# Sample queries stored one block earlier, and 44 ticks of fetched rows in memory attention instead of 35

## The chip, the core and the metric

The kernel runs on one core of one Trainium2 chip. The metric is the device time of one execution in microseconds (us), the median of several runs. One further execution was taken by the hardware profiler; it gives the rows below.

## The reference, cut to what matters

One layer of a decoder works on 1024 prompt positions and on 8 samples of 8 positions each (64 sample queries). Three branches (convolution, sparse attention, memory attention) are gated and merged, and a feed-forward net follows. The change touches two of the branches:

```python
# sparse attention of a sample: every query keeps 256 cached keys, and attends to the gathered rows
idx, valid = select_keys(indexer_scores(qi, wi, ki_all), qpos, n_sel)
kg = jnp.where(in_past, cache_k[phys, off], _gather_rows(k_new, nidx))
vg = jnp.where(in_past, cache_v[phys, off], _gather_rows(v_new, nidx))
s = jnp.einsum('nthd,ntkhd->nthk', q, kg) * (HEAD_DIM ** -0.5)
out = jnp.einsum('nthk,ntkhd->nthd', softmax(where(valid, s, NEG)), vg)
# memory attention: 4 heads, 256 memory tokens (prompt), 256 cached ones for each sample
s = jnp.einsum('nthd,nmhd->nhtm', q, mk) * (MEM_HEAD_DIM ** -0.5)
om = jnp.einsum('nhtm,nmhd->nthd', softmax(s), mv)
```

## The kernel before

The program is a row of blocks; inside a block each engine has its own list of instructions, and all engines meet at the block's end. The blocks that matter are the **products block** (projections of the input, choice of the samples' keys, memory keys and values; `second_products` is its last part, lines 1900 to 2281), the **attention block** behind it (`memory_attention`, then `prompt_attention`, line 2284 on), and the merge and feed-forward net that follow.

**Work in the attention block.** `memory_attention` has 18 steps: steps 0 to 7 take a block of 128 prompt queries each, steps 8 to 15 bring in the cached memory keys of one sample each, and steps 13 and 17 turn and mix (`sample_turn`, `sample_mix`, L1046) the values of four samples each, on PE. `prompt_attention` has 35 steps n: the pairs (b, j) with b = 0 to 7 (query block) and j = 0 to 3 (pair of heads), so n = 4b + j, and three at the end that only drain. A step of block b scores 128 queries against 128(b + 1) keys, so later steps are longer.

**Ticks.** The sparse attention of the 64 sample queries (class `Gather`, L660) is cut into 81 ticks, 0 to 80, which are spread over the steps of both attentions. A tick adds to every engine's list:

- POOL (`pool_tick`, L718): two indirect fetches (L706) of the 256 key rows of query n + 3 (tick 0 fetches for queries 0 to 3), and two (L716) for each query whose values are used in tick n + 2. The values of a group of 16 queries fall together: in ticks 18 to 28, 34 to 44, 50 to 60 and 66 to 76 of POOL. There are 256 fetches, 54 of them in ticks 50 to 60.
- DVE (`dve_tick`, `score`): the product of query n with its key rows (L880) and the sum over each head (L885). For every 16 queries it normalises a softmax. DVE also sets up the constant operands once (`dve_first`, L813 to L829).
- PE (`pe_tick`, `mix`): turns, and for each query 8 by 2 small products with its value rows (L776).
- ACT (`act_tick`): loads four queries, spread over all partitions, two groups ahead (L793).

Key rows have 5 buffers, so the fetch for query k waits for the score of query k - 5; value rows have 5 too, and the fetch for query v waits for the mix of query v - 5. `gather_ticks` (L897) sets how many ticks stand in which step: none in steps 0 to 2 of the memory attention, 3 in each of steps 3 to 7, 2 in each of steps 8 to 17 (35 in all), and the other 46 over the steps of the prompt attention in proportion to b + 2.

**Sample queries before.** At the attention block's start PE turns the 64 sample queries (`pe_first`), ACT copies them (L784) and stores them in DRAM (`q_spill`, L786), waits until they have landed, and loads the first two groups from there (`act_first`).

**End of the products block.** PE's last large work there is the memory keys and values: eight columns of products, each copied by ACT to `mkvT`, then turned and copied to `mkv` (L2049 to L2069, L2151, L2154). SP loads the memory queries (`m.omT`) and the sparse queries (`m.qT`), 2.2 MB each, once the samples' keys are coded and listed (`s_coded`, `s_listed`), and at the end waits for both loads (`queries_back`).

Of the kernel before, what the change touches and what calls it, by code (L numbers as in the profile page):

```python
# [19 lines left out]
P = 128  # L20
# [637 lines left out]
class Gather:  # L658
# [6 lines left out]
    def __init__(self, nc, m, ctx):  # L665
        self.nc, self.m = nc, m

        def sb(name, shape, dt=F32):
            return ctx.enter_context(nc.sbuf_tensor(name, shape, dt, side="right"))
        self.keys = sb("k_rows_got", [P, self.K_SLOTS, 2, DA])  # L670
        self.values = sb("v_rows_got", [P, self.V_SLOTS, 2, DA])
        self.spread = [m.room[:, R_D:R_D + 4 * DA].rearrange("p (t d) -> p t d", t=4),
                       sb("q_spread", [P, 4, DA])[:, :, :]]
        self.qtok = self.values[0:NS, self.V_SLOTS - 1, 0, :]
        self.q_bd = sb("q_bd", [P, NPAIR, 4, 32])
        self.spreadb = sb("spreadb", [P, NPAIR * P], BF16)
        self.dots = sb("satt_dots", [P, 2, 2, 4, 32])
        self.prob = sb("satt_prob", [P, self.W])
        self.pT = sb("satt_probT", [P, 8, 16, 32])
        self.pTn = sb("satt_probT_new", [NS, P])  # L680
        self.outn = sb("satt_out", [P, P])
        self.negtop, self.total = sb("satt_negtop", [P, 1]), sb("satt_total", [P, 1])
        self.k_in = [m.sem(f"k_rows_in{i}") for i in range(self.K_SLOTS)]
        self.v_in = [m.sem(f"v_rows_in{i}") for i in range(self.V_SLOTS)]
        self.q_in = [m.sem(f"q_spread_in{i}") for i in range(2)]
        self.prepared, self.set_up, self.q_turned, self.q_evac, self.q_out = (m.sem("satt_" + n) for n in (
            "zeroed", "operands", "q_turned", "q_evac", "q_out"))
        self.prod, self.dotted, self.padded, self.scored = (m.sem("satt_" + n) for n in (
            "products", "dots_s", "padded", "scores"))
        self.neg, self.weighed, self.inverted, self.normed = (m.sem("satt_" + n) for n in (  # L690
            "neg", "exp", "inverted", "normed"))
        self.turned, self.spread_out, self.v_used, self.mixed = (m.sem("satt_" + n) for n in (
            "pT", "pT_placed", "v_used", "mixed"))
        self.copied, self.out_turned, self.placed = m.sem("satt_out_copied"), m.sem("satt_out_turned"), m.sem("satt_placed")
# [29 lines left out]
        for v in self.uses(n + 2):  # L724
            self.pool_values(pool, v)

    def pe_first(self, pe):
        nc, m = self.nc, self.m
        for j in range(4):
            mm = nc.tensor.transpose(m.B[7][0:NS, j * P:(j + 1) * P], m.qT[:, j, SEQ:NT], m.ident[:, :])  # L730
        mm.then_inc(self.q_turned, 1)

    def pe_tick(self, pe, n):
        nc, m = self.nc, self.m
        i, at = n // 16 - 1, n % 16
# [2 lines left out]
            nc.tensor.transpose(m.B[7][:, 0:P], self.outn[:, :], m.ident[:, :]).then_inc(self.out_turned, 1)  # L738
        if i >= 0 and at == 0 and i < NPAIR:
            if i == 0:  # L740
                pe.wait_ge(self.q_evac, 1)
                pe.wait_ge(self.set_up, 1)
            else:
                pe.wait_ge(self.placed, 2 * i)
            pe.wait_ge(self.padded, 4 * (i + 1))
            nc.tensor.matmul(m.B[7][:, TOPK:self.W], self.spreadb[:, i * P:(i + 1) * P], m.smask[:, HALF:SW],
                             start=True, stop=False, skip_group_check=True)
            for j in range(4):
                nc.tensor.matmul(m.B[7][32 * j:32 * j + 32, TOPK:self.W], self.q_bd[:, i, j, :], m.kT[:, j, SEQ:NT],
                                 start=False, stop=True, skip_group_check=True)  # L750
            for f in range(2):
                mm = nc.tensor.transpose(m.B[7][:, f * P:(f + 1) * P],
                                         self.dots[:, i % 2, f].rearrange("p j n -> p (j n)"), m.ident[:, :])
            mm.then_inc(self.scored, 1)
# [24 lines left out]
        mm.then_inc(self.v_used, 1)  # L779

    def act_first(self, act):
        nc, m = self.nc, self.m
        act.wait_ge(self.q_turned, 1)
        nc.scalar.copy(self.qtok, m.B[7][0:NS, :]).then_inc(self.q_evac, 1)  # L784
        act.wait_ge(self.q_evac, 1)
        act.dma_start(m.q_spill[:, :], self.qtok).then_inc(self.q_out, 16)  # L786
        act.wait_ge(self.q_out, 16)
        for g in range(2):
            self.load_queries(act, g)

# [106 lines left out]
def gather_ticks():  # L897

    ticks, done = [], 0
    for i in range(QB + NSEQ + 2):  # L900
        n = 0 if i < 3 else 3 if i < QB else 2
        ticks.append(list(range(done, done + n)))
        done += n
    start = done
# [8 lines left out]
def memory_attention(nc, m, mkvT, mkv, gather, ticks):  # L913
# [4 lines left out]
    with ExitStack() as ctx:  # L918
# [55 lines left out]
        def tensor(pe):  # L974
# [73 lines left out]
                                                  start=(t == 0), stop=(t == 1))  # L1048
                    mm.then_inc(s_spv, 1)

            gather.pe_first(pe)
            for i in range(steps):
                if i in (13, 17):
                    sample_turn((i - 13) // 4)
# [15 lines left out]
        def vector(dve):  # L1070
# [53 lines left out]
            for i in range(steps):  # L1124
# [5 lines left out]
                    sample_negmax((i - 12) // 4)  # L1130
                if QB - 1 <= i < QB + NSEQ - 1:
                    half_keys(i - QB + 1)
                if i == 0:
                    gather.dve_first(dve)
                for k in ticks[i][:1]:
                    gather.dve_tick(dve, k)
                if 1 <= i <= QB:
                    half_turned(i - 1)
                if i == 2:
                    pad_queries()  # L1140
                if i in (12, 16):
                    sample_normalise((i - 12) // 4)
                for k in ticks[i][1:]:
# [762 lines left out]
def second_products(nc, m, mkvT, mkv, gemm):  # L1906


    with ExitStack() as ctx:
# [32 lines left out]
        fin = m.room[:, spare:spare + TOPK]  # L1942
        turned_rows = m.room[:, spare + TOPK:spare + 2 * TOPK]
        listed = m.room[:, spare + 2 * TOPK:spare + 2 * TOPK + 2 * NS].rearrange("p (f n) -> p f n", f=2)
        s_set, s_masked = m.sem("samp_setup2"), m.sem("sel_masked")
        s_pages, s_within, s_rows = m.sem("sel_pages_in"), m.sem("sel_within_made"), m.sem("sel_rows_turned")
        s_coded, s_listed, s_copied, s_mirror = (m.sem("sel_" + n) for n in ("coded", "listed", "copied", "mirrored"))
# [14 lines left out]
        def sync(sp):  # L1962
# [13 lines left out]
            for c in range(KD):  # L1976
# [4 lines left out]
                elif c > 4:  # L1981
                    sp.wait_ge(kv_full, c - NSLAB + 1)
                sp.dma_start(slabs[c % NSLAB], wcols(m.w_mem_kv, c * P, P)).then_inc(kv_w_in[c % NSLAB], 16)
            sp.wait_ge(s_coded, 1)
            sp.dma_start(m.omT[:, :, :], m.queries_spill[:, 0:MH, :]).then_inc(q_back, 16)
            sp.wait_ge(s_listed, 1)
            sp.dma_start(m.qT[:, :, :], m.queries_spill[:, MH:, :]).then_inc(q_back, 16)
            sp.wait_ge(kv_t_ev, 4)
            sp.dma_start(m.o_mk.rearrange("(t p) n -> p t n", p=P), mkv[:, :, 0:512]).then_inc(m.mkv_stored, 16)
# [11 lines left out]
        def tensor(pe):  # L2001
# [42 lines left out]
            for c in range(KD):  # L2044
# [3 lines left out]
                for k in range(KD):  # L2048
                    mm = nc.tensor.matmul(m.B[6 + c % 2][:, 0:NMEM].rearrange("p (t n) -> p t n", t=2),  # L2049
                                          slabs[c % NSLAB][:, k, :], memT[:, k, :, :],  # L2050
                                          start=(k == 0), stop=(k == KD - 1))
                mm.then_inc(kv_full, 1)
            pe.wait_ge(s_listed, 1)
            pe.wait_ge(gemm.emptied[0], 3 * gemm.first[-1] + 3)
            for f in range(2):
# [17 lines left out]
        def scalar(act):  # L2073
# [75 lines left out]
            for c in range(KD):  # L2149
                act.wait_ge(kv_full, c + 1)  # L2150
                nc.scalar.copy(mkvT[:, c, :], m.B[6 + c % 2][:, 0:NMEM]).then_inc(kv_ev, 1)  # L2151
            for n in range(4):
                act.wait_ge(kv_t, n + 1)
                nc.scalar.copy(mkv[:, n // 2, (n % 2) * 512:(n % 2) * 512 + 512], m.B[6 + n % 2][:, :]  # L2154
                               ).then_inc(kv_t_ev, 1)
            for s in range(2):
                act.wait_ge(gate_out[s], 16 * (NR + 1))
                act.wait_ge(gemm.emptied[s], 3 * gemm.first[-1] + 3)
            act.wait_ge(c_out, 16)

        def vector(dve):
            link = Link(dve, s_set)
# [974 lines left out]
```

## Time and profile before

| | us |
|---|---|
| median of 3 runs (lowest, highest) | 2384.75 (2384.69, 2387.75) |
| profiled execution: its time | 2387.08 |
| profiled execution: its span | 2385.5 |

| engine | busy us | share of the span |
|---|---|---|
| PE (matmul) | 2187.4 | 92% |
| PEld (weight load) | 2012.3 | 84% |
| DVE | 1309.2 | 55% |
| POOL | 808.6 | 34% |
| ACT | 601.5 | 25% |

The shares are means over the whole span. The attention block lies between 912 us and some 1323 us, and its shares differ from these: a window of the trace gives the busy time of each engine in one stretch. A row of a timeline has the start in us, the duration, the engine, line and operation, and in brackets the idle time before it and what ended that. "SPq" and "ACTq" are the DMA issues of those engines.

### The profile page before, as it was taken

To read this page: it belongs to the slowest core of one execution; us is meant where nothing else is said; L and a number is where in the kernel's file an instruction comes from. 1 tells how busy PE (TensorE), PEld (TensorE's weight loads), DVE (VectorE), ACT (ScalarE), POOL (GpSimd) and SP (SyncE) were. 2 spreads that over 40 slices of the span, in tenths; PEclk is the share of its full clock that TensorE was granted. 3 is DMA by queue.
4 is the path that set the end of the run, shared out by engine and by line. 5 is a ranking of instruction groups with operands and counts; after the bars stand their busy time and mean duration, and the time that the engine had idled before them with its cause. 6 is when DMAs were issued, how large, how long until landed. Compare 5 with 4: busy or idle time off the path is not lost. (4 is left out here: it accounts for less than half of the span.)

```text
span 2385.5 us, 36459 instructions
## 1 busy us (share of the span) xinstructions
PE 2187.4 (92%) x14030; PEld 2012.3 (84%) x14030; DVE 1309.2 (55%) x1981; ACT 601.5 (25%) x1050; POOL 808.6 (34%) x591
## 2 busy tenths in 40 slices
PE   5978999999999996568779899999999999999997
PEld 5938887889999995445456799989999999999997
DVE  5078999999789996846774445331111121211123
ACT  4152222232242214303334212222111111111112
POOL 5103333221212213777773124433222322232221
PEclk9989999999999998867889899999999999999999
DMA  5102222333322245988773445211111111111112
GB/s 174 39 23 76 63 53 69 92 110 109 100 102 92 90 144 219 322 289 267 227 231 103 148 133 161 82 45 35 44 47 51 42 40 51 44 37 47 48 31 97
DMA packets 231682, 249.15 MB, mean 104 GB/s; under 512 B 37283, under 2 KB 192976, under 8 KB 228989
## 3 DMA queue, kind: packets, MB, share of 16 engines
q1 hardware_dynamic: 184974, 129.15, 17.9%
q0 software_dynamic: 23552, 70.28, 9.3%
q10 hardware_dynamic: 23031, 48.07, 5.5%
q8 instruction: 77, 1.26, 0.2%
q14 instruction: 48, 0.39, 0.1%
HBM read 212.37 MB, written 35.43 MB: 104 GB/s over the span
## 5 line engine op out<-in xcount | busy, mean ns | idle before, releaser
L419 POOL TENSOR_TENSOR ffn_w_lo<-ffn_w_raw,ffn_w_hi 128x1024 fp32r<-128x1024 f32 (+2 forms) x108 | 220.1, 2038 | 520.8 <-ACT ffn_w_hi L203 520.8
L397 PE MATMUL banks<-h_hi,in_w_hi 128*128 128x384 f32 (+1 forms) x1056 | 349.7, 331 | 7.2 <-PEq L1808 7.2
L399 PE MATMUL banks<-h_hi,in_w_lo 128*128 128x384 f32 (+1 forms) x1056 | 345.8, 327 | 0.0
L398 PE MATMUL banks<-h_lo,in_w_hi 128*128 128x384 f32 (+1 forms) x1056 | 345.5, 327 | 0.0
L397 PE MATMUL banks<-ffn_in_hi,ffn_w_hi 128*128 128x384 f32 (+1 forms) x1032 | 339.1, 329 | 5.3 <-POOL ffn_w_lo L419 3.8
L398 PE MATMUL banks<-ffn_in_lo,ffn_w_hi 128*128 128x384 f32 (+1 forms) x1032 | 338.6, 328 | 0.0
L399 PE MATMUL banks<-ffn_in_hi,ffn_w_lo 128*128 128x384 f32 (+1 forms) x1032 | 338.6, 328 | 0.0
L397 PE MATMUL banks<-halves,ffn_w_hi 128*128 128x384 f32 (+1 forms) x822 | 269.4, 328 | 11.0 <-DVE halves L2587 11.0
L399 PE MATMUL banks<-halves,ffn_w_lo 128*128 128x384 f32 (+1 forms) x822 | 269.5, 328 | 0.0
L398 PE MATMUL banks<-halves,ffn_w_hi 128*128 128x384 f32 (+1 forms) x822 | 269.4, 328 | 0.0
L419 POOL TENSOR_TENSOR in_w_lo<-in_w_raw,in_w_hi 128x1024 fp32r<-128x1024 f32 x48 | 127.0, 2648 | 386.8 <-ACT in_w_hi L203 386.8
L397 PEld LDWEIGHTS banks<-h_hi,in_w_hi 128*128 128x128 f32 x1056 | 199.2, 189 | 21.9 <-issue 21.7
L397 PEld LDWEIGHTS banks<-ffn_in_hi,ffn_w_hi 128*128 128x128 f32 x1032 | 194.9, 189 | 6.1 <-issue 4.0
L398 PEld LDWEIGHTS banks<-h_lo,in_w_hi 128*128 128x128 f32 x1056 | 199.1, 189 | 0.4 <-issue 0.2
L399 PEld LDWEIGHTS banks<-h_hi,in_w_lo 128*128 128x128 f32 x1056 | 199.1, 188 | 0.0
L398 PEld LDWEIGHTS banks<-ffn_in_lo,ffn_w_hi 128*128 128x128 f32 x1032 | 195.0, 189 | 0.0
L203 ACT CAST ffn_w_hi<-ffn_w_raw 128x1024 fp32r<-128x1024 f32 (+2 forms) x108 | 94.2, 873 | 399.4 <-PE banks L399 300.4
L399 PEld LDWEIGHTS banks<-ffn_in_hi,ffn_w_lo 128*128 128x128 f32 x1032 | 194.9, 189 | 0.0
L706 POOL DMA_INDIRECT k_rows_got<-in_cache_k,sel_row x128 | 136.3, 1065 | 113.9 <-POOLq L2997 54.1
L1240 DVE SCALAR_TENSOR_TENSOR room<-room,w_dw 128x1024 f32<-128x1024 f32 x120 | 171.7, 1492 | 1.1
L397 PEld LDWEIGHTS banks<-halves,ffn_w_hi 128*128 128x128 f32 x822 | 155.2, 189 | 11.2 <-DVE halves L2587 11.2
L1749 DVE TENSOR_SCALAR_CACHE_REDUCE mask<-room,sel_cand 128x384 bf16<-128x384 f32 (+1 forms) x186 | 163.7, 942 | 1.1
(385 smaller groups left out, 3851.3 us busy)
## 6 DMA issues: line engine op xcount, KB each, us to landing
in_w_raw<-in_w_in SPq DMA_DIRECT2D x48, 512.0 KB, 3.9
ffn_w_raw<-in_w_ffn_in SPq DMA_DIRECT2D x44, 512.0 KB
merge_gate<-gate_spill_dram SPq DMA_DIRECT2D x24, 544.0 KB, 3.8
ffn_w_raw<-in_w_ffn_out SPq DMA_DIRECT2D x24, 384.0 KB
gate_spill_dram<-second_out ACTq DMA_DIRECT2D x16, 544.0 KB, 2.7
room<-q_spill_dram ACTq DMA_DIRECT2D x8, 1024.0 KB, 7.3
q_spread<-q_spill_dram ACTq DMA_DIRECT2D x8, 1024.0 KB, 7.8
gate_spill_dram<-first_out ACTq DMA_DIRECT2D x8, 544.0 KB, 2.8
```

Of the source, the lines that this page charges most:

```text
L203: self.m.nc.scalar.copy(self.w_hi[:, s, 0:g.kc, :], self.raw[:, s, 0:g.kc, :]).then_inc(self.hi_done, 1)
L397: nc.tensor.matmul(out, self.w_hi[:, s, k, :], g.hi[:, k, a:a + w], start=(k == 0), stop=False)
L398: nc.tensor.matmul(out, self.w_hi[:, s, k, :], g.lo[:, k, a:a + w], start=False, stop=False)
L399: mm = nc.tensor.matmul(out, self.w_lo[:, s, k, :], g.hi[:, k, a:a + w], start=False, stop=(k == g.kc - 1))
L419: self.m.nc.gpsimd.tensor_tensor(self.w_lo[:, s, 0:g.kc, :], self.raw[:, s, 0:g.kc, :], self.w_hi[:, s, 0:g.kc, :], ALU.subtract).then_inc ...
L706: pool.indirect_dma_start(self.keys[:, n % self.K_SLOTS, f, :], None, rows, bass.IndirectOffsetOnAxis(ap=m.sel_row[:, f, n:n + 1], axis=0) ...
L1240: nc.vector.scalar_tensor_tensor(out=dst, in0=src, scalar=m.wdw[:, c, k:k + 1], in1=dst, op0=ALU.mult, op1=ALU.add).then_inc(tap, 1)
L1749: c = nc.vector.tensor_scalar(m.mask[:, MOFF[b]:MOFF[b + 1]], sl(b), lim, 0.0, op, ALU.add, accum_out=cnt[:, j:j + 1])
```

## The change

Four edits:

1. The turn of the sample queries, their copy and their store move from the attention block's start to the end of the products block. SP loads the 64 sample queries there (`q_rows`), PE turns them behind the last memory product, ACT makes four copies to free pieces of buffers (`q_tok`) and four stores. The load of `m.qT` now waits for these stores (one piece of `q_tok` lies in its place), and ACT's end of block too.
2. `act_first` only loads the first two groups.
3. `dve_first` moves from step 0 to step 2 of the memory attention, behind `pad_queries`.
4. `gather_ticks` puts 2, 3, 4, 3, 3, 3, 3, 3 ticks into steps 0 to 7 (24) and 2 into each of steps 8 to 17 (20): 44 in all, and 37 in the prompt attention.

```diff
@@ class Gather
-        self.qtok = self.values[0:NS, self.V_SLOTS - 1, 0, :]
...
     def act_first(self, act):
-        nc, m = self.nc, self.m
-        act.wait_ge(self.q_turned, 1)
-        nc.scalar.copy(self.qtok, m.B[7][0:NS, :]).then_inc(self.q_evac, 1)
-        act.wait_ge(self.q_evac, 1)
-        act.dma_start(m.q_spill[:, :], self.qtok).then_inc(self.q_out, 16)
-        act.wait_ge(self.q_out, 16)
         for g in range(2):
             self.load_queries(act, g)
@@ gather_ticks
-    for i in range(QB + NSEQ + 2):
-        n = 0 if i < 3 else 3 if i < QB else 2
+    for n in (2, 3, 4) + 5 * (3,) + 10 * (2,):
         ticks.append(list(range(done, done + n)))
@@ memory_attention, vector
-                if i == 0:
-                    gather.dve_first(dve)
                 for k in ticks[i][:1]:
                     gather.dve_tick(dve, k)
                 if 1 <= i <= QB:
                     half_turned(i - 1)
                 if i == 2:
                     pad_queries()
+                    gather.dve_first(dve)
@@ second_products
+        at = spare + 2 * TOPK + 2 * NS
+        q_rows = m.room[:, at:at + 4 * NS].rearrange("p (j n) -> p j n", j=4)
+        q_tok = [(0, m.room[0:NS, R_B + 2 * HALF:R_B + 2 * HALF + 2 * P]),
+                 (2 * P, m.room[0:NS, at + 4 * NS:at + 4 * NS + P]),
+                 (3 * P, gate[0:NS, 0, SEQ:NT]), (3 * P + NS, gate[0:NS, 1, SEQ:NT])]
...
+                if c == 4:
+                    sp.wait_ge(s_cent, 3 * KC)
+                    sp.dma_start(q_rows, m.queries_spill[:, MH:, SEQ:NT]).then_inc(q_got, 16)
             sp.wait_ge(s_coded, 1)
             sp.dma_start(m.omT[:, :, :], m.queries_spill[:, 0:MH, :]).then_inc(q_back, 16)
             sp.wait_ge(s_listed, 1)
+            sp.wait_ge(q_out, 16 * len(q_tok))
             sp.dma_start(m.qT[:, :, :], m.queries_spill[:, MH:, :]).then_inc(q_back, 16)
...
+            pe.wait_ge(q_got, 16)
+            pe.wait_ge(gemm.emptied[1], 3 * gemm.first[-1] + 3)
+            for j in range(4):
+                mm = nc.tensor.transpose(m.B[3][0:NS, j * P:(j + 1) * P], q_rows[:, j, :], m.ident[:, :])
+            mm.then_inc(q_turned, 1)
             pe.wait_ge(s_listed, 1)
...
                 nc.scalar.copy(mkvT[:, c, :], m.B[6 + c % 2][:, 0:NMEM]).then_inc(kv_ev, 1)
+            for s in range(2):
+                act.wait_ge(gate_out[s], 16 * (NR + 1))
+            act.wait_ge(c_out, 16)
+            act.wait_ge(q_turned, 1)
+            for a, to in q_tok:
+                nc.scalar.copy(to, m.B[3][0:NS, a:a + to.shape[1]]).then_inc(q_placed, 1)
+            act.wait_ge(q_placed, len(q_tok))
+            for a, to in q_tok:
+                act.dma_start(m.q_spill[:, a:a + to.shape[1]], to).then_inc(q_out, 16)
             for n in range(4):
```

SP's queue at the end of the products block. `queries_spill_dram` is the source of all three loads; the two of 128x4352 are `m.omT` and `m.qT`. Before:

```order
L1983 DMA memkv_w<-in_w_mem_kv 128x8x128 [waits memkv_full]
L1983 DMA in_w_raw<-in_w_mem_kv 128x8x128 [waits memkv_full] x2
L1985 DMA room<-queries_spill_dram 128x4352 [waits sel_coded]
L1987 DMA room<-queries_spill_dram 128x4352 [waits sel_listed]
L1989 DMA out_o_mk<-mkv 128x2x512 [waits mkv_evac]
L1990 DMA out_o_mv<-mkv 128x2x512
L1874 UNCONDITIONAL_BRANCH [waits queries_back,sel_pages_in]
```

With the change:

```order
L1974 DMA room<-queries_spill_dram 128x4x64 [waits conv_centered]
L1971 DMA memkv_w<-in_w_mem_kv 128x8x128 [waits memkv_full]
L1971 DMA in_w_raw<-in_w_mem_kv 128x8x128 [waits memkv_full] x2
L1976 DMA room<-queries_spill_dram 128x4352 [waits sel_coded]
L1979 DMA room<-queries_spill_dram 128x4352 [waits sample_q_stored,sel_listed]
L1981 DMA out_o_mk<-mkv 128x2x512 [waits mkv_evac]
L1982 DMA out_o_mv<-mkv 128x2x512
L1856 UNCONDITIONAL_BRANCH [waits queries_back,sel_pages_in]
```

The load of the sample queries is new, and the second large load has a second wait, for the sample queries' store (`sample_q_stored`); the two stores of memory keys and values stand behind it.

ACT's list at the same place, with the change (before, the eight copies of `mkvT` are followed at once by the four of `mkv`):

```order
L2148 COPY mkvT<-banks 128x256 [waits memkv_full] x8
L2154 COPY room<-banks 64x256 [waits conv_spilled,sample_q_turned,second_spilled1,second_spilled0]
L2154 COPY room<-banks 64x128
L2154 COPY second_out<-banks 64x64 x2
L2157 DMA q_spill_dram<-room 64x256 [waits sample_q_placed]
L2157 DMA q_spill_dram<-room 64x128
L2157 DMA q_spill_dram<-second_out 64x64 x2
L2160 COPY mkv<-banks 128x512 [waits mkv_turned] x4
```

The four copies and four stores are new here. The second and the last two stores have rows of 128 and 64 floats.

DVE's list from the attention block's start. Before, up to the first score:

```order
L1080 TENSOR_REDUCE mem_negtop<-banks 128x2 x2
L813 MEMSET spreadb 128x256
L814 MEMSET q_bd 128x512
L815 MEMSET satt_probT 128x4096
L823 COPY q_bd<-room 64x4x8 x16
L829 TENSOR_SCALAR spreadb<-ident 64x16x8 x4
L1073 RECIPROCAL mem_total<-mem_total 128x4
...
L1104 MEMSET room 128x1024
L1109 COPY room<-room 128x4x8 x8
L1073 RECIPROCAL mem_total<-mem_total 128x4
L1080 TENSOR_REDUCE mem_negtop<-banks 128x2 x2
L880 TENSOR_TENSOR k_rows_got<-k_rows_got,room 128x1024
```

With the change:

```order
L1063 TENSOR_REDUCE mem_negtop<-banks 128x2 x2
L865 TENSOR_TENSOR k_rows_got<-k_rows_got,room 128x1024
L870 TENSOR_REDUCE satt_dots<-k_rows_got 128x8x2
L865 TENSOR_TENSOR k_rows_got<-k_rows_got,room 128x1024
L870 TENSOR_REDUCE satt_dots<-k_rows_got 128x8x2
L1056 RECIPROCAL mem_total<-mem_total 128x4
L1063 TENSOR_REDUCE mem_negtop<-banks 128x2 x2
...
L1092 COPY room<-room 128x4x8 x8
L798 MEMSET spreadb 128x256
L799 MEMSET q_bd 128x512
L800 MEMSET satt_probT 128x4096
L808 COPY q_bd<-room 64x4x8 x16
```

The first score (L880 before, L865 now) stands behind the first two reductions instead of in step 3, nine ticks stand in steps 0 to 2, and the set-up of the constants stands behind them.

## Rows read from the trace of the kernel before

**Rows 1.** Windows: busy us (instructions) of PE, PEld, DVE, ACT, POOL; PE clock, DMA share, GB/s.

```profile
1170.00:1252.00 82.00, 63.86 (x683) 44.49 (x681) 61.17 (x84) 27.95 (x59) 62.28 (x63) 0.89 0.74 226
1252.00:1323.00 71.00, 61.14 (x752) 44.02 (x748) 30.04 (x49) 26.92 (x50) 20.77 (x22) 0.96 0.31 90
```

**Rows 2.** Timeline of POOL in the attention block.

```profile
912.72 1.01 POOL L706 DMA_INDIRECT k_rows_got<-in_cache_k,sel_row  x1 [54.12 <-POOLq L2997]
...
940.32 0.94 POOL L706 DMA_INDIRECT k_rows_got<-in_cache_k,sel_row  x1 [14.56 <-DVE satt_dots L885]
...
989.63 0.95 POOL L706 DMA_INDIRECT k_rows_got<-in_cache_k,sel_row  x1 [0.70 <-DVE satt_dots L885]
...
1167.80 1.12 POOL L706 DMA_INDIRECT k_rows_got<-in_cache_k,sel_row  x1 [0.71 <-DVE satt_dots L885]
...
1238.07 0.95 POOL L716 DMA_INDIRECT v_rows_got<-in_cache_v,sel_row  x1 [0.30 <-issue]
...
1271.21 0.95 POOL L716 DMA_INDIRECT v_rows_got<-in_cache_v,sel_row  x1 [19.26 <-PE banks L776]
```

**Rows 3.** Timelines around the end of the products block: PE, SP's queue, ACT.

```profile
902.79 2.54 PE L2049 MATMUL banks<-mkv,in_w_raw 128*128 128x256 f32 x11
...
909.35 0.47 SPq L1990 DMA_DIRECT2D out_o_mv<-mkv  x1
...
911.95 0.90 SPq L947 DMA_DIRECT2D memc_k<-in_cache_mem_k  x2
...
913.06 0.58 ACT L784 COPY v_rows_got<-banks 64x512 f32<-64x512 f32 x1 [4.18 <-PE banks L730]
```

**Rows 4.** DMA issues: KB each where shown, median us to landing, some in windows.

```profile
room<-queries_spill_dram SPq DMA_DIRECT2D x1, 2176.0 KB, 9.6
...
room<-queries_spill_dram SPq DMA_DIRECT2D x1, 2176.0 KB, 7.8
...
gate_spill_dram<-second_out ACTq DMA_DIRECT2D x16, 544.0 KB, 2.7
...
q_spill_dram<-v_rows_got ACTq DMA_DIRECT2D x1, 128.0 KB, 6.2
...
k_rows_got<-in_cache_k,sel_row POOLq DMA_INDIRECT x24, 6.1
...
v_rows_got<-in_cache_v,sel_row POOLq DMA_INDIRECT x128, 3.8
```

**Rows 5.** Timeline of DVE: the first score, and the last instruction of tick 16.

```profile
937.57 1.22 DVE L880 TENSOR_TENSOR k_rows_got<-k_rows_got,room 128x1024 f32<-128x1024 f32 x1
...
988.14 1.22 DVE L885 TENSOR_REDUCE satt_dots<-k_rows_got 128x16 f32<-128x1024 f32 x1
```

**Rows 6.** Windows, columns as in rows 1: DVE's set-up, and the padding of queries.

```profile
917.09:924.39 7.30, 0.39 (x2) 0.00 (x0) 6.39 (x23) 3.21 (x9) 5.78 (x6) 0.82 1.05 416
933.85:935.57 1.72, 1.72 (x13) 1.59 (x12) 1.69 (x10) 1.72 (x8) 0.00 (x0) 1.00 0.00 0
```

**Rows 7.** Timelines around the second sample mix: ACT behind it, PE's entry to prompt attention.

```profile
1084.05 0.27 ACT L1202 COPY room<-banks 128x128 f32<-128x128 f32 x1 [13.91 <-PE banks L1046]
...
1086.20 0.42 PE L2330 MATMUL banks<-mask,bigident 128*128 128x128 bf16 x2
```

**Rows 8.** Timelines of prompt attention: ACT's exponentials (L2481), and one of PE's mixes.

```profile
1122.14 0.58 ACT L2481 ACTIVATE att_prob<-banks,att_negtop 128x384 f32<-128x384 f32 x1 [1.28 <-DVE att_negtop L2403]
...
1171.55 0.79 ACT L2481 ACTIVATE att_prob<-banks,att_negtop 128x640 f32<-128x640 f32 x1 [3.77 <-DVE att_negtop L2403]
...
1176.72 0.79 ACT L2481 ACTIVATE att_prob<-banks,att_negtop 128x640 f32<-128x640 f32 x1 [1.97 <-DVE att_negtop L2403]
...
1248.77 0.65 PE L776 MATMUL banks<-v_rows_got,satt_probT 128*32 128x128 f32 x16
...
1254.58 1.01 ACT L2481 ACTIVATE att_prob<-banks,att_negtop 128x896 f32<-128x896 f32 x1 [3.00 <-DVE att_negtop L2403]
...
1261.65 1.01 ACT L2481 ACTIVATE att_prob<-banks,att_negtop 128x896 f32<-128x896 f32 x1 [2.72 <-DVE att_negtop L2403]
```

More of the change, by code:

```diff
@@ L685, in __init__ @@
         self.q_in = [m.sem(f"q_spread_in{i}") for i in range(2)]
-        self.prepared, self.set_up, self.q_turned, self.q_evac, self.q_out = (m.sem("satt_" + n) for n in (
-            "zeroed", "operands", "q_turned", "q_evac", "q_out"))
+        self.prepared, self.set_up = m.sem("satt_zeroed"), m.sem("satt_operands")
         self.prod, self.dotted, self.padded, self.scored = (m.sem("satt_" + n) for n in (
@@ L725, in pool_tick @@
             self.pool_values(pool, v)
-    def pe_first(self, pe):
-        nc, m = self.nc, self.m
-        for j in range(4):
-            mm = nc.tensor.transpose(m.B[7][0:NS, j * P:(j + 1) * P], m.qT[:, j, SEQ:NT], m.ident[:, :])
-        mm.then_inc(self.q_turned, 1)
     def pe_tick(self, pe, n):
@@ L740, in pe_tick @@
             if i == 0:
-                pe.wait_ge(self.q_evac, 1)
                 pe.wait_ge(self.set_up, 1)
@@ L781, in act_first @@
     def act_first(self, act):
-        nc, m = self.nc, self.m
-        act.wait_ge(self.q_turned, 1)
-        nc.scalar.copy(self.qtok, m.B[7][0:NS, :]).then_inc(self.q_evac, 1)
-        act.wait_ge(self.q_evac, 1)
-        act.dma_start(m.q_spill[:, :], self.qtok).then_inc(self.q_out, 16)
-        act.wait_ge(self.q_out, 16)
         for g in range(2):
@@ L1049, in sample_mix @@
                     mm.then_inc(s_spv, 1)
-            gather.pe_first(pe)
             for i in range(steps):
@@ L1944, in second_products @@
         listed = m.room[:, spare + 2 * TOPK:spare + 2 * TOPK + 2 * NS].rearrange("p (f n) -> p f n", f=2)
+        at = spare + 2 * TOPK + 2 * NS
[3 more added lines that the diff above has]
+                 (3 * P, gate[0:NS, 0, SEQ:NT]), (3 * P + NS, gate[0:NS, 1, SEQ:NT])]
+        q_got, q_turned, q_placed, q_out = (m.sem("sample_q_" + n) for n in ("back", "turned", "placed", "stored"))
         s_set, s_masked = m.sem("samp_setup2"), m.sem("sel_masked")
@@ L2156, in scalar @@
             for s in range(2):
-                act.wait_ge(gate_out[s], 16 * (NR + 1))
                 act.wait_ge(gemm.emptied[s], 3 * gemm.first[-1] + 3)
-            act.wait_ge(c_out, 16)
+            act.wait_ge(q_out, 16 * len(q_tok))
         def vector(dve):
```

## The prediction

> **What bounds the kernel now.** The page's first part says PE, 92% of the span; but that is a mean over stages, and the change lies in the attention block alone. So I read the windows next [rows 1]. From 1170 to 1252 PE is busy 63.9 of 82 us, DVE 61.2 and POOL 62.3: no engine is full. From 1252 to 1323, the tail of the prompt attention, POOL is busy 20.8 of 71 and DVE 30.0, and PE 61.1. The first stretch waits for something that the second does not.
>
> POOL's timeline names it [rows 2]. A fetch takes 0.95 us and the next starts 0.30 later without any wait, so no fetch costs less than 1.25 us of POOL. Between the fetch at 1167.80 (the first of tick 50, released by the score of query 48) and the one at 1238.07 (the last of tick 60) lie 54 fetches in 71.2 us, 1.32 each: POOL is issuing all the time. Its last value rows land 3.8 us later [rows 4], at 1242.8, and PE's last mix of that group ends at 1249.4 [rows 8], in tick 62, which stands in step n = 24 of the prompt attention. Behind it the sign turns: POOL waits 19.26 us for PE [rows 2]. So the **time of the attention block is POOL's stream up to tick 60, and then what PE still has to do behind tick 62**. The stream itself starts at 912.72, waits 14.56 us for the first score until 940.32, and from 989.63 (tick 18, where the value fetches begin) it runs nearly without waits.
>
> The change therefore has three places: when the stream starts, where it gets a new wait, and how much of the prompt attention is left when it lets PE go.
>
> **1. The boundary.** Before, the attention block opens at 911.95, when SP issues its first load there [rows 3], 2.1 us after its last issue in the block before had ended (909.35 + 0.47 = 909.82). The load of `m.qT` was off this path. Now it waits for the stores of the sample queries, and the block's end waits for it. The chain: the last memory product ends at 902.79 + 2.54 = 905.3 [rows 3]. Four turns of 64 columns follow; no row shows them alone, but before they ran between the block's start and the ACT copy at 913.06, so 1.1 us at most: 906.4. Four ACT copies: the one of all 512 columns took 0.58, so between 0.58 and 2.3 together; I take 1.1, since the pieces hold as many columns together: 907.5. Four issues at 0.47, the last one begun 1.4 later: 908.9. The landing: a small ACT store of this kernel lands in 2.7 at the median, the old store of these very rows took 6.2, with other loads running [rows 4]; I take 2.7, since at this place only the block's last loads run: 911.6. `m.qT`, 2.2 MB, took 7.8 and its twin 9.6 [rows 4]; I take 8.7: 920.3. Plus 2.1: the block opens at 922.4, **+10.5 us**. With both lower ends of copies, landing and load it is +9, with the upper ends +15.5.
>
> Two of the four stores and the new load on SP move pieces of 64 floats, 256 bytes; no row shows what such pieces cost a store here. The Trainium skill, "DMA: Bandwidth & Descriptors", section Specifications, says that transfers under 512 bytes are done as read-modify-write and don't reach line rate. The page gives no price for it; if it moved the landing to the upper end, the sum below would be 3.5 us higher. That is a rule against this change, which no run shows yet; the sum goes without it.
>
> **2. The front of the memory attention.** Before, the first score starts at 937.57 [rows 5], 25.6 us after the block opens, and tick 16 ends at 988.14 + 1.22 = 989.36: 51.8 us for 17 ticks with DVE's other work of steps 3 to 8. Now the first score needs its keys (second fetch issued at 2.1, landing 6.1 [rows 4]: 8.2) and its queries (7 to 8, issued at once as act_first no longer waits). So it starts 9 us after the opening, and 2 more are lost while the loads of the block's start share the 16 DMA engines, which are full then (share 1.05, 416 GB/s, [rows 6]). From there to the end of tick 16 DVE does the same 17 ticks, and between them the set-up, 7.3, and the padding, 1.7 [rows 6], which before lay ahead of the first score; one step less of other work takes about 0.7 off. 51.8 + 7.3 + 1.7 - 0.7 = 60. The end of tick 16 is then 9 + 2 + 60 = 71 us behind the opening, before it was 77.4. **So the front gains about 7**, of the 16 that the first score gains. The bounds: nothing, if DVE stands for the loads for 9 instead of 2, and 9, if for none. POOL's tick 18 comes at +10.5 - 7 = **+3.5**: the early ticks have not quite paid for the boundary.
>
> **3. The end of the memory attention.** The stream stays at +3.5 while nothing stops it. In step 17 PE now mixes the values of tick 41 first, whose fetches are 94 behind the start of tick 18. From there to tick 50 POOL issued 128 fetches in 178.2 us before [rows 2], 1.39 each: 993.1 + 94 x 1.39 + 3.8 = 1127.6. Only behind them on PE's list stands the second sample mix, which held ACT's next copy up for 13.91 us [rows 7], then three mixes of ticks 42 and 43 at 0.65 [rows 8]. PE enters the prompt attention at about 1143.5, before at 1086.2 [rows 7]. That is no loss by itself: nine ticks fewer are left.
>
> **4. The prompt attention up to tick 62.** Before, PE's entry to the exponential of n = 9 takes 1122.14 - 1086.2 = 36 us [rows 8], with seven ticks in it; now five, so 34. In n = 9 stands tick 48, whose score releases tick 50 of POOL: 1177.5, against 1167.80, **+10**. So the new wait is PE's late entry, and the stream, +3.5 until then, loses 6.5 to it. Ticks 50 to 60 have 54 fetches as before: + 71.2 = 1249.3, + 3.8 = 1253, and the mix of tick 62 ends at 1254, +4.6 against 1249.4; less than +10, since PE was itself late behind the rows before.
>
> **5. What is left.** With 37 ticks in place of 46, tick 62 stands in step n = 21 instead of 24 (94/182 x 37 = 19 ticks are out by then). So three steps more lie behind the stream: n = 22 and 23 with 768 keys, n = 24 with 896. Exponential to exponential took 5.17 with 640 keys and 7.07 with 896 [rows 8]; I take 6.1, 6.1 and 7.0, **+19**. The 18 ticks behind tick 62 lie on 13 steps in place of 10, so the tail has fewer stops: -3, of the 5 by which its 73.6 us (1249.4 to 1323) exceed its steps.
>
> **Sum:** 4.6 + 19 - 3 = +20.6 on the profiled execution's 2387.1, which is 2407.7; the median of the runs shown is 2.3 below that execution, so the forecast is **2405** for the median. The merge and the feed-forward net are untouched and follow the block's end.
>
> **The rivals.** All times are against 2384.75.
>
> - *A second bind at the sample mixes* (slower still). A mix holds PE for 14 us in steps 13 and 17, in bursts of value fetches with five buffers; the fetch for query v waits for the mix of v - 5. Before, the bursts lay elsewhere to these mixes. If the buffers are full, POOL loses up to 14 at each, and what it loses in step 17 moves tick 50 and all behind it: with one full loss 2405 + 14 = 2419. For: ticks 34 to 44 now run in steps 12 to 17. Against: five buffers are some 13 us of fetches, so most of it is covered.
> - *No bind in the prompt attention* (about the same). If POOL is well ahead, PE goes at its own pace: 34 to n = 9, then two steps at 4.5, four at 4.6, four at 5.2, four at 6.1, one at 7: 113 from 1143.5, so n = 24 ends at 1256, +7; with the 3 to 5 of the tail, +2 to +4, 2388. It decides whether 54 fetches need longer than the twelve steps from n = 9 to n = 21, about 60 us: at 1.25 each they take 67.5, and that speaks against it.
> - *The tail goes by its ticks, not by its steps* (faster). If the 73.6 us behind tick 62 come from its 18 ticks, 4.1 us each, three more steps cost nothing. With the lower end of the boundary and of the front, the stream is at -1 and tick 62 ends 3 to 4 earlier, and the tail loses 3: -6, 2379. It decides whether steps n = 22 to 24 run beside the ticks. Against: POOL's 19.26 us of waiting for PE there, and DVE busy 30 of 71 us.
>
> **How the numbers follow.** A measurement of this kernel can tell about 0.2%, 4.8 us, from no change. Forecast 0.60, range 2394 to 2416 (boundary +9 to +15.5, front 0 to 9, most of both absorbed in step 4, steps at 5.2 to 7.1 each); worse at the mixes 0.16; no bind 0.12, of which 0.08 within 0.2%; ticks in the tail 0.12, of which 0.10 faster and 0.02 within. Faster 0.10, same 0.10, slower 0.80. The range 2388 to 2421 leaves out the faster cases and half of the worst.
>
> **What would show it.** The block's first SP load near 922, with the load of `m.qT` ending last before it; the first score some 11 us later; POOL's tick 18 near 993; PE's entry near 1143.5; the first fetch of tick 50 near 1177, released by a score; tick 62's mix near 1254; the prompt attention's end near 1343. The forecast is wrong if tick 50 starts before 1170, if POOL waits for PE's mixes for over 10 us ahead of it, or if less than 85 us pass from tick 62's mix to the end.

## The result, and the profile after

| | before | changed |
|---|---|---|
| median, us | 2384.72 | 2413.99 |
| lowest to highest, us | 2381.74 to 2387.75 | 2413.64 to 2416.38 |
| profiled execution, its time | 2387.08 | 2413.7 |

The changed kernel is **slower**, by 1.2%: ratio 1.0121, 95% interval 1.0106 to 1.0136, which is 29.3 us between the medians and 26.6 between the profiled executions (forecast: 20.6). The working below goes by the profiled ones.

SP's queue at the boundary, changed kernel (timeline):

```profile
910.31 0.34 SPq L1979 DMA_DIRECT2D room<-queries_spill_dram  x1
911.50 0.39 SPq L1981 DMA_DIRECT2D out_o_mk<-mkv  x1
911.93 0.66 SPq L1982 DMA_DIRECT2D out_o_mv<-mkv  x1
921.15 0.89 SPq L931 DMA_DIRECT2D memc_k<-in_cache_mem_k  x2
```

DMA issues of the same kernel from 895 to 925 (KB each, median us to landing):

```profile
room<-queries_spill_dram SPq DMA_DIRECT2D x1, 2176.0 KB, 8.7
...
q_spill_dram<-room ACTq DMA_DIRECT2D x1, 64.0 KB, 1.9
...
q_spill_dram<-second_out ACTq DMA_DIRECT2D x2, 16.0 KB, 1.8
```

The load of `m.qT` leaves at 910.31, when the stores have landed, and takes 8.7 us; the attention block opens at 921.15 against 911.95 before [rows 3]: **+9.2**.

POOL's timeline, changed kernel, the fetches that answer to [rows 2], and one more with a long wait:

```profile
921.93 1.01 POOL L704 DMA_INDIRECT k_rows_got<-in_cache_k,sel_row  x1 [63.35 <-POOLq L3002]
...
962.55 1.68 POOL L704 DMA_INDIRECT k_rows_got<-in_cache_k,sel_row  x1 [10.38 <-DVE satt_dots L870]
...
992.97 0.95 POOL L704 DMA_INDIRECT k_rows_got<-in_cache_k,sel_row  x1 [0.61 <-DVE satt_dots L870]
...
1176.44 0.94 POOL L704 DMA_INDIRECT k_rows_got<-in_cache_k,sel_row  x1 [7.51 <-DVE satt_dots L870]
...
1286.51 0.94 POOL L714 DMA_INDIRECT v_rows_got<-in_cache_v,sel_row  x1 [23.87 <-PE banks L767]
```

The 14.56 us of waiting at the start are gone, but tick 8 waits 10.38 for the score of query 6, which stands behind the set-up in DVE's list (the set-up lies behind six of the nine early ticks, not behind all of them as was told ahead). Tick 18 starts at 992.97, 3.3 later than before, and tick 50 at 1176.44, 8.6 later, with the new wait of 7.51 for a score.

PE's timeline, changed kernel: the second half of the second sample mix, the entry to prompt attention, the mix of tick 62, and the turns that every first step of a query block has:

```profile
1131.50 6.98 PE L1030 MATMUL banks<-mem_sprobT,mem_prob 128*128 128x8 f32 x32
...
1141.13 0.40 PE L2335 MATMUL banks<-mask,bigident 128*128 128x128 bf16 x2
...
1251.21 1.16 PE L767 MATMUL banks<-v_rows_got,satt_probT 128*32 128x128 f32 x32
...
1273.24 2.05 PE L2366 MATMUL banks<-ident,att_inverse 128*128 128x128 f32 x8 [2.07 <-ACT att_probT L2470]
```

ACT's exponentials of n = 22 to 25, changed kernel:

```profile
1258.02 0.90 ACT L2486 ACTIVATE att_prob<-banks,att_negtop 128x768 f32<-128x768 f32 x1 [4.22 <-DVE att_negtop L2408]
...
1264.83 0.90 ACT L2486 ACTIVATE att_prob<-banks,att_negtop 128x768 f32<-128x768 f32 x1 [2.54 <-DVE att_negtop L2408]
...
1271.52 1.01 ACT L2486 ACTIVATE att_prob<-banks,att_negtop 128x896 f32<-128x896 f32 x1 [3.00 <-DVE att_negtop L2408]
...
1283.02 1.01 ACT L2486 ACTIVATE att_prob<-banks,att_negtop 128x896 f32<-128x896 f32 x1 [3.00 <-DVE att_negtop L2408]
```

PE enters the prompt attention at 1141.13, 54.9 later than before, and ends tick 62's mix at 1252.4, 3.0 later. Behind it n = 22 to 24 take 25.0 us, from 1258.02 to 1283.02.

The view that sorts all of this best is PE's busy time in two windows, from the block's opening to PE's entry, and from there to the end of the prompt attention (columns as in rows 1). Before:

```profile
911.95:1086.20 174.25, 109.47 (x813) 90.86 (x814) 115.72 (x168) 46.92 (x135) 121.09 (x114) 0.72 0.81 280
1086.20:1319.00 232.80, 190.00 (x2040) 125.65 (x2038) 150.43 (x229) 81.15 (x191) 146.42 (x143) 0.89 0.63 199
```

Changed:

```profile
921.15:1141.13 219.98, 123.65 (x1009) 103.18 (x1010) 139.23 (x192) 46.72 (x134) 161.59 (x152) 0.69 0.80 276
1141.13:1345.50 204.37, 173.44 (x1843) 115.98 (x1839) 127.31 (x203) 81.09 (x191) 105.90 (x104) 0.94 0.53 167
```

PE does the same work (299.5 and 297.1 us in all), and waits elsewhere: 64.8 and 42.8 us before (174.25 less 109.47, and so on), **96.3 and 30.9** now. So its waiting in the memory attention grew by 31.5 and that in the prompt attention shrank by only 11.9. With 2.4 us less busy, that is +17.3 (424.35 us for the two windows together, 407.05 before); the boundary's 9.2 make it +26.5, the profiles' difference but for 0.1.

The view of who waits for whom (us in total, times, longest) says what PE waits for in the memory attention. Before:

```profile
PE banks L1003 <- ACT mem_prob L1161: 29.7, 7, 8.9
PE banks L776 <- DMA v_rows_got<-in_cache_v,sel_row: 28.6, 11, 8.0
```

Changed:

```profile
PE banks L767 <- DMA v_rows_got<-in_cache_v,sel_row: 44.6, 15, 7.0
PE banks L987 <- ACT mem_prob L1143: 44.1, 7, 14.4
```

Fetched value rows account for 16.0 us more. Another 14.4 are waits for the softmax of the memory attention, in which ACT waits for DVE: the early scores and the set-up stand ahead of its steps in DVE's list, and ACT waits there 8.59 us until 936.84 and 13.71 until 967.17. In the prompt attention, PE's waits for fetched rows fell from 16.9 to 8.8 us.

### The profile page after: what moved, and what is told of

Read it like the earlier page. It is cut to its first block and busy times, and to the rows that moved or that the text cites. A ratio compares the mean times of both kernels' runs of the same rounds, so it can differ in the third digit from the quotient of the medians.

```text
span 2412.1 us, 36469 instructions
## 1 busy us (share of the span) xinstructions
PE 2185.9 (91%) x14030; PEld 2015.5 (84%) x14030; DVE 1309.6 (54%) x1981; ACT 601.7 (25%) x1053; POOL 808.9 (34%) x591
## 5 line engine op out<-in xcount | busy, mean ns | idle before, releaser
L704 POOL DMA_INDIRECT k_rows_got<-in_cache_k,sel_row x128 | 131.4, 1027 | 125.1 <-POOLq L3002 63.3
L397 PEld LDWEIGHTS banks<-halves,ffn_w_hi 128*128 128x128 f32 x822 | 155.2, 189 | 11.5 <-DVE halves L2592 11.5
```

Of the source, the lines that this page charges most:

```text
L397: nc.tensor.matmul(out, self.w_hi[:, s, k, :], g.hi[:, k, a:a + w], start=(k == 0), stop=False)
L704: pool.indirect_dma_start(self.keys[:, n % self.K_SLOTS, f, :], None, rows, bass.IndirectOffsetOnAxis(ap=m.sel_row[:, f, n:n + 1], axis=0) ...
```

## The experiments

The theory at first was the prediction's: POOL's stream up to tick 60 and the steps behind tick 62 set the end. The profiles reach the end of the products block up to 4.4 us apart, so places are counted from each kernel's own opening of the attention block (SP's first load there), where that is said.

### The three parts of the change, one at a time

`e1_old_table`: the change with the old table.

```diff
-    for n in (2, 3, 4) + 5 * (3,) + 10 * (2,):
+    for i in range(QB + NSEQ + 2):
+        n = 0 if i < 3 else 3 if i < QB else 2
```

> The change with the old table of ticks (none in steps 0 to 2, 35 in the memory attention, 46 in the prompt attention); the early store of the sample queries and the later set-up stay. Theory: the boundary's 9.2 us shift the whole POOL stream and nothing else differs from before: tick 18 near 999, tick 62 in n = 24 near 1258.6, some 69 us behind it, so 2394 us. Rival, that the boundary carries the loss and the early ticks give some of it back: the front gain of 6 is lost on top, 2414 to 2420.

Measured: 2398.21, ratio 1.0051 (1.0034 to 1.0068). The block opens at 921.77, and tick 50 starts at 1179.69, 11.9 later than before: the boundary's 9.8 and 2.0 more, part of which is a first score that comes 1.3 later against the opening. Everything behind is shifted as a whole, PE's entry too (1097.89, 11.7 later). The boundary passes to the end in full; it is not the larger part of the change's 29.

`e2_old_store`: the kernel before with the new table, and `dve_first` in step 2.

> The kernel before with the new table and the set-up in step 2; the sample queries are turned and stored at the attention block's start, as before. Theory: the block opens at 912 again, but the first score waits for the queries' store and load and starts near 928; tick 18 near 989, PE enters prompt attention near 1138, tick 62 stays in n = 21 and some 93 us follow it: 2408 to 2412 us. Rival, that the boundary carries the loss: 9 us or more come back, 2405 or less.

Measured: 2408.8, ratio 1.0103 (1.0086 to 1.012). The block opens at 909.25, tick 18 starts at 986.74, 77.5 behind that (before 77.7, changed kernel 71.8). PE enters at 1133.74, 224.5 behind the opening, against 174.3 before. So the table, without the early store, costs 23.0 us, where the early store without the table costs 12.4; and the early store is worth 5.7 us at the front. What the early ticks gain there depends on the place of the set-up: `e5_early_35` below has the same ticks in steps 0 to 7 and the same old store, but the set-up in step 0, and its tick 18 starts 69.4 behind the opening.

`e3_free_piece`: the change, with the first copied piece moved out of `m.qT`'s place.

```diff
-        q_tok = [(0, m.room[0:NS, R_B + 2 * HALF:R_B + 2 * HALF + 2 * P]),
+        q_tok = [(0, m.room[0:NS, R_D:R_D + 2 * P]),
...
-            sp.wait_ge(q_out, 16 * len(q_tok))
             sp.dma_start(m.qT[:, :, :], m.queries_spill[:, MH:, :]).then_inc(q_back, 16)
...
             act.wait_ge(q_turned, 1)
+            act.wait_ge(s_listed, 1)
```

> The change, but the first copied piece of the sample queries lies in a place that the load of m.qT doesn't overwrite, and that load doesn't wait for the stores. Theory: the block opens near 913.5 in place of 921.2, everything behind moves by the same 7.6 us, and the tail of 93 us stays: 2406 us. Rival, that the boundary is most of the loss: 2395 or less.

Measured: 2407.64, ratio 1.0098 (1.0081 to 1.0115), near the 2406 expected. SP's timeline shows the load of `m.qT` off the path, 15.1 us ahead of the opening:

```profile
897.15 0.34 SPq L1978 DMA_DIRECT2D room<-queries_spill_dram  x1
...
909.66 0.47 SPq L1981 DMA_DIRECT2D out_o_mv<-mkv  x1
912.28 0.89 SPq L931 DMA_DIRECT2D memc_k<-in_cache_mem_k  x2
```

Before, that load was issued 12.4 us ahead of the opening:

```profile
899.52 0.34 SPq L1987 DMA_DIRECT2D room<-queries_spill_dram  x1
```

So 2.7 of the boundary's 9.2 us stay without the new wait, in the row of `out_o_mv`, which comes that much later behind the load than before (12.5 us against 9.8 [rows 3]) and waits for ACT's copies of `mkv`; the wait ahead of the load costs the other 6.5.

### Is it the place of tick 62?

`e4_tail_steps`: the change, prompt ticks placed by hand, tick 62 in n = 24.

```diff
-    weight = [b + 2 for b in range(QB) for _ in range(HEADS // 2)] + [2, 2, 2]
...
+    where = (0, 2, 3, 4, 5, 7, 9, 11, 12, 13, 14, 16, 17, 18, 19, 20, 22, 23, 24, 24, 25, 25, 26, 26, 27, 27, 28, 28, 29, 29, 30, 30, 30, 31, 31, 33, 34)
+    for n in range(4 * QB + 3):
+        ticks.append([done + k for k, at in enumerate(where) if at == n])
```

> The change, with the 37 ticks of the prompt attention put elsewhere: ticks 44 to 49 in steps 0 to 7, tick 62 in n = 24, and all ticks behind it in the steps in which they stood before. Theory: tick 50 of POOL starts near 1171 instead of 1176, tick 62's mix ends near 1253 to 1256, and 69 to 73 us follow it instead of 93: 2392 to 2398 us. Rival, that the tail goes by its ticks or that the tail's extra time isn't the three steps: 2409 to 2414.

Measured: 2410.29, ratio 1.0103 (1.0085 to 1.0121), no difference from the change that could be measured. Tick 50 did start 5.1 sooner against the opening. But the exponential of n = 24 then stands at 1264.62, 125.7 behind PE's entry at 1138.9:

```profile
1264.62 1.01 ACT L2483 ACTIVATE att_prob<-banks,att_negtop 128x896 f32<-128x896 f32 x1 [3.00 <-DVE att_negtop L2405]
```

In the change it was 130.4 behind the entry (1271.52). PE cannot be in n = 24 when the rows of tick 62 land: the miss falls on the first theory. A second one took its place: **the prompt attention of the change runs almost at PE's own pace, and its end is PE's late entry plus that pace**.

`e12_half_fetch` leaves out 48 of POOL's fetches and so sets the two against each other:

```diff
-        for f in range(2):
+        for f in range(1 if n >= 48 else 2):
             pool.indirect_dma_start(self.keys[:, n % self.K_SLOTS, f, :], None, rows,
...
-        for f in range(2):
+        for f in range(1 if v >= 32 else 2):
             pool.indirect_dma_start(self.values[:, v % self.V_SLOTS, f, :], None, rows,
```

> The change, with the second fetch of the key rows left out for queries 48 to 63 and of the value rows for queries 32 to 63 (the products then run on the rows that lie there): 48 fetches, some 60 us of POOL, fewer. If POOL's stream up to tick 60 sets the change's end, tick 62 comes up to 30 us sooner and so does the end: 2380 to 2386. If the prompt attention of the change runs at PE's own pace from its late entry, as e4_tail_steps suggests, only the wait in n = 18 goes, some 10 us: 2401 to 2408.

Measured: 2400.94, ratio 1.0069 (1.0054 to 1.0085): some 12 us less than the change, and not 30. The windows, and PE's waits for fetched rows in the second one:

```profile
919.57:1140.20 220.63, 121.02 (x1009) 99.67 (x1009) 139.20 (x192) 46.77 (x134) 162.49 (x152) 0.69 0.81 274
...
1140.20:1332.20 192.00, 168.00 (x1843) 113.34 (x1839) 127.23 (x203) 81.20 (x191) 60.56 (x57) 0.97 0.36 114
...
PE banks L770 <- DMA v_rows_got<-in_cache_v,sel_row: 0.8, 1, 0.8
```

With POOL busy 60.6 us in place of 105.9, PE still needs 192.0 us for the prompt attention, 12.4 less than in the change, and enters it as late behind the opening (220.6 and 220.0). It waits only 0.8 us for fetched rows there, in place of 8.8. That is its pace with 37 ticks and a stream that is out of the way, and it shows the second theory: the stream accounts for some 12 us of the change's prompt attention, and the rest of the loss was made before PE came in.

### Where ticks may stand

`e8_39_ticks`: 15 ticks in place of 20 in steps 8 to 17 (`5 * (1, 2)`), else the change.

> The change with 15 instead of 20 ticks in steps 8 to 17, so 39 instead of 44 in the memory attention and 42 behind, by the old weights. Theory: PE enters prompt attention near 1110 instead of 1141; the stream to tick 60 runs without the wait at tick 50; tick 62 lies in n = 23 in place of 21, so about half of the table's loss comes back: 2394 to 2402 us. Rival, that the loss is the late stream alone: 2405 to 2414.

Measured: 2405.26, ratio 1.0076 (1.0059 to 1.0093): a miss, above the 2394 to 2402 expected and at the lower end of the rival's range. PE entered 23 us sooner than in the change (1117.68), and 0.45% came back of the 0.70% that lie between the ratios of the change and of e1. POOL waited 9.72 us for a score at tick 34, and tick 50 started at 1179.83, 3.6 later against the opening than in the change: the theory's stream without a wait was wrong here.

`e5_early_35`: the kernel before, early ticks but 35 in all.

```diff
-    for i in range(QB + NSEQ + 2):
-        n = 0 if i < 3 else 3 if i < QB else 2
+    for n in (2, 3, 4) + 5 * (3,) + 9 * (1,) + (2,):
```

> The kernel before with 24 ticks in steps 0 to 7 (2, 3, 4, 3, 3, 3, 3, 3) and 11 in steps 8 to 17, 35 in all as before; the store of the queries and the set-up stay where they were, so the set-up lies in the wait for the queries. Theory (the time goes by POOL's stream up to tick 60 plus the same tail): tick 18 comes 7 to 9 us earlier against the block's start, the stream stays that much ahead, the tail is as before: 2376 to 2379 us. Rival, that early ticks only move the wait elsewhere: 2385.

Measured: 2394.03, ratio 1.003 (1.002 to 1.0039): a miss, slower than the rival's 2385 too. Tick 18 did come 8.3 us sooner against the opening, without any early store. POOL's timeline shows where that went:

```profile
1069.08 1.68 POOL L706 DMA_INDIRECT k_rows_got<-in_cache_k,sel_row  x1 [12.13 <-DVE satt_dots L885]
...
1094.67 0.95 POOL L706 DMA_INDIRECT k_rows_got<-in_cache_k,sel_row  x1 [6.63 <-DVE satt_dots L885]
```

With one tick in a step, the scores of ticks 30 and 34 stand too late in DVE's list, and POOL waits 18.8 us for them. What is taken early is missing later.

`e6_timed_prompt`: the kernel before with its 46 prompt ticks in later steps (list of steps as in e4, tick 46 in n = 16, tick 62 in n = 28).

> The kernel before with the same 35 ticks in the memory attention; the other 46 stand in the prompt step that PE reaches, at the pace of e4_tail_steps (which waited for POOL nowhere for long), when their rows have landed: tick 46 in n = 16, tick 62 in n = 28, and not n = 14 and 24. Theory (PE's entry plus its own pace of some 213 us up to the merge, and before 31 us of waits for POOL on top): the waits go, the stream stays as it was; merge near 1300 to 1306 instead of 1330, 2354 to 2362 us. Rival, that POOL's stream and the tail of 70 us behind tick 62 set the time wherever the ticks stand: 2380 to 2386.

Measured: 2379.1, ratio 0.9961 (0.9947 to 0.9975): faster than before, but by 8 to 9 us of the 25 to 33 that were expected, and just below the rival's 2380 to 2386. POOL still waits for PE ahead of the last value rows:

```profile
1273.64 0.94 POOL L716 DMA_INDIRECT v_rows_got<-in_cache_v,sel_row  x1 [14.32 <-PE banks L776]
```

`e9_chain_early`: as e6, ticks 63 and 64 in n = 27, 65 to 68 in n = 28, and those behind them earlier.

> e6_timed_prompt with the last softmax, ticks 63 to 68, in steps 27 and 28 instead of 28 to 30, and five earlier ticks one step sooner; nothing else. In e6 the value stream of the last group began at 1273.64, as late as before (1271.21), with POOL waiting 14.3 us for PE there. Theory: that wait goes, the stream's end and the merge come 8 to 16 us sooner than in e6: 2363 to 2371 us. Rival, that PE's own pace is the end already: 2376 to 2380.

Measured: **2372.77, ratio 0.9947 (0.9933 to 0.9961)**, the lowest median of all, between the two expectations; the interval overlaps that of e6. The reason given for it does not hold: that fetch starts at 1271.85, with a wait of 16.31 in front, 361.9 us behind the opening; in e6 it was 361.7.

`e7_both` (e5 and e6 together):

> Both: 24 of the 35 ticks early and the prompt ticks timed. Theory: PE's entry 5 to 7 us earlier with the stream, the rest as in e6: 2348 to 2357 us. Rival: as e5, 2376.

Measured: 2382.44, ratio 0.9983 (0.9973 to 0.9993): a miss, and above the rival's 2376. POOL waits 9.42 and 6.66 us at ticks 32 and 36, as in e5.

`e10_early_spaced`: e9 with `(2, 3, 4) + 5 * (3,) + (1, 1, 1, 1, 1, 1, 3, 2, 0, 0)`.

> e9_chain_early with the early ticks of e5 (24 in steps 0 to 7, store and set-up where they were before), but the 11 others in steps 8 to 15 (1, 1, 1, 1, 1, 1, 3, 2) and none in steps 16 and 17, so that the scores of ticks 30 to 34 aren't behind the sample mix; in e5 POOL waited 12.1 and 6.6 us for them. Theory: those waits go, the stream stays 8 us ahead of before's against the block's start, PE enters as early, and the end comes 5 to 8 us sooner than in e9: 2356 to 2365 us. Rival, that the early ticks' gain is lost again whatever the spacing: no sooner than e9.

Measured: 2377.62, ratio 0.9976 (0.9963 to 0.9989). The waits only shrank, to 7.79 and 6.9 us (ticks 32 and 37), and PE entered 183.9 behind the opening against 174.8 in e9. The rival stands: the early ticks' gain was lost again.

`e11_free_early`: e10 with the store of e3 and the set-up in step 0.

> e10_early_spaced with the change's early store in the form of e3_free_piece (no wait ahead of m.qT's load) and the set-up in step 0, in the wait for the first rows. Theory: the block opens within 1 us of before against the last products, the first score comes 5 us sooner than in e10, tick 18 too: 0 to 5 us less than e10. Rival, that the store's copies and issues cost at the block's end what the first score gains: as e10 or up to 3 us more.

Measured: 2378.62, ratio 0.9975 (0.9962 to 0.9987), as e10. Tick 18 comes 66.4 behind the opening in place of 69.7, but the opening comes 15.9 behind the issue of `m.qT`'s load in place of 12.4: the early store takes at the block's end what it gives at the first score.

## Why the prediction was right, and where it was not

The sign, the range and most places held; the sum was 6 us short on the profiled executions (20.6 forecast, 26.6 measured). The medians (2405 forecast, 2413.99 measured) lie 9 apart, since the forecast took 2.3 off for the median, and the changed kernel's profiled execution is no longer than its median.

- **Boundary.** +10.5 was forecast, +9.2 measured. The landing of the stores was priced at 2.7 us and took 1.9; `m.qT`'s load took the 8.7 that was chosen.
- **Front.** The block's first score comes 10.6 behind the opening (11 was forecast), tick 18 at 992.97 (993), with the set-up's price visible as the 10.38 us at tick 8. That tick 18 fits so well is luck: the boundary came out 1.3 lower than forecast, and the front gained 5.9 (77.7 less 71.8) and not 7.
- **Entry.** 1141.13 (1143.5). POOL did not lose 14 us at the sample mixes: the first rival is out.
- **Tick 50.** 1176.44 (1177.5), released by a score, as forecast. **Tick 62:** 1252.4 (1254).
- **What is left: the term that was mis-sized.** "I take 6.1, 6.1 and 7.0, +19" measured 6.8, 6.7 and 11.5, **25.0**. All three were priced as steps inside a query block. But n = 24 is the first step of one, with eight turns more and a wait for ACT ahead of them (2.05 and 2.07 us in the row at 1273.24). Before had it too: its exponential of n = 24 stood at 1244.53, and that of n = 25 at 1254.58 [rows 8], 10.1 apart; the 7.07 that was used is the step from there on.
- **The tail.** -3 was forecast. From the exponential of n = 25 to the first product of the merge it is 73.8 in place of 75.4, -1.6. So tick 62 came 1.6 sooner than forecast, the tail gave back 1.4 less, and the two nearly cancel: this, too, is luck.

So 3.0 + 25.0 - 1.6 and 0.5 for where the mix stands in its step make, up to rounding, the 26.8 by which the merge starts later (1356.78 against 1329.98).

The step n = 24 before, from its exponential to that of n = 25 (timelines of ACT and PE, window as in rows 1):

```profile
1244.53 1.01 ACT L2481 ACTIVATE att_prob<-banks,att_negtop 128x896 f32<-128x896 f32 x1 [4.69 <-DVE att_negtop L2403]
...
1246.25 1.13 PE L2361 MATMUL banks<-ident,att_inverse 128*128 128x128 f32 x8 [2.07 <-ACT att_probT L2465]
...
1244.53:1254.58 10.05, 7.95 (x81) 5.63 (x83) 8.23 (x13) 4.01 (x8) 5.52 (x6) 1.00 0.66 190
```

The same step in the changed kernel:

```profile
1271.52:1283.02 11.50, 9.02 (x67) 6.83 (x69) 3.92 (x8) 4.25 (x9) 0.00 (x0) 0.85 0.00 0
```

It is 1.4 longer, at a mean granted clock of 0.85 in place of 1.00, and the eight turns took 2.05 us in place of 1.13 behind the same wait of 2.07. The ticks in it differ too, and no run separates the two.

The reading behind the sum was half right. For the kernel before, that POOL's stream sets the time is likely but not shown: PE waits 16.9 us for fetched rows in its prompt attention, and e6, which put the ticks into later steps, won 8 to 9 us and not 25 to 33; but e1, 12.4 longer with a stream 11.9 us later, moved PE's entry by 11.7 as well. For the changed kernel e12 shows that the stream holds up the prompt attention by only 12.4 us. That was the second rival, "no bind in the prompt attention", whose own pace was priced too low, by the same first steps of blocks among others: it gave 113 us from the entry to the end of n = 24, and e12, with next to no waiting for fetched rows, had its exponential of n = 24 at 1260.64, 120.4 behind the entry, and that of n = 25 at 1271.22, 131.0 behind it. The stream up to tick 60 and PE's own pace from a late entry came out within 12.4 us of each other, so the sum came out near by either road; that it did is luck. What cost the time is the same in both: nine more ticks stand between PE and the prompt attention, which PE could have worked on while POOL fetched. The third rival, the tail going by its ticks, is out: the three steps took their full time.

Open: whether e9 is faster than e6 beyond the noise, and if so why, with its last group's fetches at the same place; and whether a table exists in which the early ticks keep their 8 us.

## What to carry to other kernels

Where a slow stream (here POOL's fetches) feeds an engine with a fixed order of work, more of the stream's work ahead of a stage does not make the stream faster; it makes the engine wait there. Count the busy engine's waiting by stage, before and after: here PE's busy time went from 299 to 297 us, and the loss inside the attention block is all in where it waits. A small store in front of a large load at a block's end put the load's 8.7 us on the path here, though the store takes 1.9, and the wait between them cost 6.5 (e3); and a step is priced over a whole round, with its first and last member, not from one typical pair of rows.

## What was not expected of the hardware

Stores with rows of 64 floats landed in 1.8 us, no later than the one with rows of 256 floats (1.9). The Trainium skill, "DMA: Bandwidth & Descriptors", section Specifications, says that transfers below 512 bytes are done as read-modify-write and don't reach line rate; for stores of 16 KB no price of it shows here.

The same work took PE different times. The prompt attention has the same 1843 products in three kernels. They are busy for 168.0 us in e12, where the mean granted clock is 0.97, for 173.4 in the change at 0.94, and for 175.2 in e4 at 0.92 (window from 1138.90 to 1340.50). So of the 12.4 us that e12 saves in this stage, 5.4 are the same products done faster, and 6.9 are waits. The low clock lies in single stretches, as at e4's entry:

```profile
1138.90:1148.90 10.00, 3.64 (x47) 2.20 (x45) 2.84 (x4) 1.07 (x5) 7.81 (x8) 0.67 1.01 382
...
1148.90:1158.90 10.00, 9.39 (x68) 5.16 (x68) 7.18 (x14) 3.51 (x15) 7.09 (x7) 0.50 0.90 337
```

PE was busy 3.64 of the first 10 us, with a wait of 5.71 for fetched rows, and in the next 10, busy for 9.39, it was granted 0.50 throughout, the lower of the two levels (1.2 of 2.4 GHz). But the sum of the waits does not order the kernels: e4 waits 26.4 us in this stage and the change 30.9, and e4 has the lower clock.
